# Experts taken in an order set by their token counts, two products instead of three for up and down in every second one, and every seventh weight remainder made by GpSimd

## The reference

```python
def moe_swiglu(h, w_router, w_gate, w_up, w_down):
    """Top-2-of-8 routed SwiGLU (softmax over the selected logits)."""
    logits = (h @ w_router).astype(jnp.float32)
    top_val, top_idx = lax.top_k(logits, TOP_K)
    top_w = jax.nn.softmax(top_val, axis=-1)
    ...
    for e in range(N_EXPERTS):
        y = swiglu(h, w_gate[e], w_up[e], w_down[e])
        out = out + gates[..., e:e + 1].astype(h.dtype) * y
    return out
```

## Time and profile before

| | us |
|---|---|
| median of 3 runs | 1777.85 (1777.68 to 1777.86) |
| span of the profiled execution | 1775.3 |
| TensorE matmuls busy | 1761.8 |
| VectorE busy | 1402.3 |
| ScalarE busy | 1141.6 |
| GpSimd busy | 134.5 |
| the experts | from about 443.5 to 1423 |

### The profile page before, as it was taken

One profiled execution on the slowest core, in us unless ns is written; L12 is line 12 of the kernel. 1 busy time (PEld: TensorE's weight loads), 2 busy tenths in 40 slices (PEclk: granted clock), 3 DMA queues, 4 the chain that ended last, 5 costly groups with the idle time before them and its releaser, 6 DMA issues.

```text
span 1775.3 us, 25580 instructions
## 1 busy us (share of the span) xinstructions
PE 1761.8 (99%) x9850; PEld 1525.6 (86%) x9850; DVE 1402.3 (79%) x1179; ACT 1141.6 (64%) x974; POOL 134.5 (8%) x142
## 2 busy tenths in 40 slices
PE   9999999999999999999999999999999999999999
PEld 8889999998888888888888888888888889789998
DVE  7475545655988989889889889898898879878775
ACT  6444433563777778777778777777777646756553
POOL 7000000000110000000000000000000017610000
PEclk9999999999999999999999999999999999999999
DMA  7447555542999999998999989999989943416561
GB/s 259 150 145 233 168 193 189 168 142 99 347 378 329 378 378 343 385 370 321 379 373 359 376 318 375 369 355 388 367 322 378 329 159 123 139 65 221 168 212 48
DMA packets 244645, 479.27 MB, mean 270 GB/s; under 512 B 11791, under 2 KB 80169, under 8 KB 244537
## 3 DMA queue, kind: packets, MB, share of 16 engines
q1 hardware_dynamic: 243673, 476.43, 75.1%
q10 hardware_dynamic: 864, 1.31, 0.2%
HBM read 476.66 MB, written 1.05 MB: 269 GB/s over the span
## 4 chain that ended last, share of the span: by engine, by line
PE 91%; DVE 4%; POOL 2%; ACT 1%; issue 1%; DMA 0%; DVEq 0%; ACTq 0%; SPq 0%; POOLq 0%
PE bank L2140 26%; PE bank L2142 26%; PE bank L2141 26%; PE bank L2648 1%; PE bank L2254 1%; PE bank L2262 1%; PE bank L2255 1%; PE bank L2591 1%; POOL arena L857 1%; POOL arena L856 1%; DVE xT L1410 1%; DVE wl L449 0%; PE bank L2436 0%; PE bank L2440 0%; PE bank L2437 0%
## 5 line engine op out<-in xcount | busy, mean ns | idle before, releaser
L1652 DVE TENSOR_TENSOR wl<-raw,wh 128x2048 fp32r<-128x2048 f32 x224 | 514.6, 2304 | 89.3 <-ACT wh L1082 88.1
L1082 ACT ACTIVATE wh<-raw 128x2048 fp32r<-128x2048 f32 x224 | 429.7, 1919 | 131.8 <-PE bank L2142 126.5
L2140 PE MATMUL bank<-wh,xTh 128*128 128x512 f32 x1000 | 395.9, 396 | 0.1
L2142 PE MATMUL bank<-wh,xTl 128*128 128x512 f32 x1000 | 389.8, 390 | 0.0
L2141 PE MATMUL bank<-wl,xTh 128*128 128x512 f32 x1000 | 389.1, 389 | 0.0
L449 DVE TENSOR_TENSOR wl<-raw,wh 128x2048 fp32r<-128x2048 f32 x112 | 254.8, 2292 | 65.4 <-ACT wh L442 63.6
L2140 PE MATMUL bank<-xTh,wh 128*128 128x256 f32 x944 | 268.0, 284 | 0.2 <-DVE wl L449 0.2
L2142 PE MATMUL bank<-xTh,wl 128*128 128x256 f32 x944 | 267.1, 283 | 0.0
L2141 PE MATMUL bank<-xTl,wh 128*128 128x256 f32 x944 | 267.1, 283 | 0.0
L1652 DVE TENSOR_TENSOR wl<-arena,wh 128x2048 fp32r<-128x2048 f32 x112 | 255.2, 2284 | 0.0
L1082 ACT ACTIVATE wh<-arena 128x2048 fp32r<-128x2048 f32 x112 | 215.3, 1922 | 50.4 <-PE bank L2142 50.3
(11 more groups left out here) (450 smaller groups left out, 2078.0 us busy)
## 6 DMA issues: line engine op xcount, KB each, us to landing
raw<-in_moe_w_up SPq DMA_DIRECT2D x112, 1024.0 KB, 7.6
arena<-in_moe_w_gate SPq DMA_DIRECT2D x96, 1024.0 KB, 7.4
raw<-in_moe_w_down SPq DMA_DIRECT2D x96, 1024.0 KB, 7.0
raw<-in_w_up SPq DMA_DIRECT2D x22, 1024.0 KB, 5.2
raw<-in_moe_w_gate SPq DMA_DIRECT2D x16, 1024.0 KB, 7.4
arena<-in_moe_w_down SPq DMA_DIRECT2D x16, 1024.0 KB, 7.1
raw<-in_gla_w_in SPq DMA_DIRECT2D x12, 1024.0 KB, 7.5
raw<-in_w_in SPq DMA_DIRECT2D x12, 1024.0 KB, 6.5
```

The lines of the kernel that those rows point to most:

```text
L1082: V.activation(wh[:, s, :], src, ACT.Copy).then_inc(sg("hi_moe"), 1)
L1652: V.tensor_tensor(wl[:, s, :], moe_raw(c)[0], wh[:, s, :].bitcast(F32), ALU.subtract).then_inc(lo_moe, 1)
L2140: T.matmul(o, xh, yh, start=first, stop=False)
L2142: return T.matmul(o, xl, yh, start=False, stop=last)
```

## The change

Four things are changed together.

1. After the router, VectorE sorts the experts by their counts. Expert 0 stays first; of the other seven, the four with the fewest tokens take the second place of the four pairs, the rest the first places. Gates and places in `pm` are permuted by the same matrix, and SyncE reads the number of the expert to load from `order_i`.
2. The second expert of a pair has 64 places (`CAP`). Its one-hot repeats the 64 columns, so that the gathered tile holds the tokens twice. For up and down the stationary operand is now 64 columns of the high part beside 64 columns of the low part (`BOTH`), and `mm2` multiplies it by w_high and by w_low: two matmuls in place of three. Gate keeps three. The two halves of the up result are added when the activation is turned, as a matmul with `fold`, and the halves of the down result when it is added back.
3. A further pass of four pairs runs where an expert has more than 128 tokens or at least four of experts 1 to 7 have more than 64.
4. Pieces c with c % 42 % 7 == 5 (six of an expert's 42) have their remainder made by GpSimd, which counts them in a semaphore of its own; its four `xnl` remainders are placed ahead of the first four of them. On GpSimd some small constants are added early in the kernel.

```diff
-        xTh = sb("xTh", [P, KD, S], F32R)
-        xTl = sb("xTl", [P, KD, S], F32R)
+        xhl = sb("xhl", [P, 2, KD, S], F32R)
+        xTh, xTl = xhl[:, 0], xhl[:, 1]
...
+        lo_moe_pool = sg("lo_pool")
+        pool_makes = [c % UC % 7 == 5 for c in range(PC)]
+        N_POOL = sum(pool_makes)
+        assert not any(pool_makes[0:NW])
+
         def moe_split(eng, at, c):
 
-            eng.wait_ge(lo_moe, at(PC, c + 1))
+            same = [k for k in range(c % PC + 1) if pool_makes[k] == pool_makes[c % PC]]
+            n = N_POOL if pool_makes[c % PC] else PC - N_POOL
+            eng.wait_ge(lo_moe_pool if pool_makes[c % PC] else lo_moe, at(n, c // PC * n + len(same)))
...
+        CAP = (P, P // 2)
+
         def slots(i):
 
             return slice((1 - i % 2) * P, (2 - i % 2) * P)
+
+        def tokens_of(i):
+
+            return xhl[:, 1 - i % 2]
+
+        HIGH, LOW, BOTH = slice(0, P), slice(P, 2 * P), slice(P // 2, 3 * P // 2)
+
+        def turned_act(i):
+
+            return bank[4][:, 0:4 * CAP[i]].rearrange("p (k s) -> p k s", k=4)
...
-                load_expert(c, 0)
+                load_expert(c, (0, 0))
             sp.wait_ge(sg("more_ready"), 1)
             more = sp.value_load(more_i[0:1, 0:1], min_val=0, max_val=NPAIR)
+            sp.wait_ge(sg("more_ready"), 2)
+
+            def expert_at(u):
+                return sp.value_load(order_i[0:1, bass.ds(u, 1)], min_val=0, max_val=NE - 1)
+
             with sp.Fori(0, more + (NPAIR - 1)) as p:
-                e = (p % NPAIR) * 2
+                e = expert_at(2 * (p % NPAIR)), expert_at(2 * (p % NPAIR) + 1)
                 for c in range(NRX, PC):
                     moe_split(sp, lambda a, b: p * a + b, c - NRX)
                     load_expert(c, e)
-                e2 = ((p + 1) % NPAIR) * 2
+                e2 = (expert_at(2 * ((p + 1) % NPAIR)),)
...
+            def weight_low(at, c):
+                s = (M0 + c) % NW
+                pool.wait_ge(sg("hi_moe"), at(PC, c + 1))
+                V.tensor_tensor(wl[:, s, :], moe_raw(c)[0], wh[:, s, :].bitcast(F32), ALU.subtract).then_inc(lo_moe_pool, 1)
+
+            mine = [c for c in range(PC) if pool_makes[c]]
+            for n, c in enumerate(mine):
+                if n < 4:
+                    pool.wait_ge(sg("moe_used"), 6 * n + 4 - 3 * (n > 0))
+                    xn_low(n)
+                weight_low(lambda a, b: b, c)
+            more = pool.value_load(more_i[0:1, 0:1], min_val=0, max_val=NPAIR)
+            with pool.Fori(0, more + (NPAIR - 1)) as p:
+                for c in mine:
+                    weight_low(lambda a, b: p * a + (a + b), c)
...
                 s = (M0 + c) % NW
+                if pool_makes[c % PC]:
+                    return
...
                 pmu = pm[:, bass.ds(u, 1), :].rearrange("p a t -> p (a t)")
-                V.tensor_tensor(oh2[:, :, slots(i)], iota2, pmu.unsqueeze(2).to_broadcast([P, TT, P]), ALU.is_equal).then_inc(sg("moe_oh"), 1)
+                n = CAP[i % 2]
+                shape = [P, TT, P // n, n]
+                V.tensor_tensor(oh2[:, :, slots(i)].rearrange("p t (a s) -> p t a s", s=n),
+                                iota[:, 0:n].unsqueeze(1).unsqueeze(1).to_broadcast(shape),
+                                pmu.unsqueeze(2).unsqueeze(3).to_broadcast(shape), ALU.is_equal).then_inc(sg("moe_oh"), 1)
...
+            C(V.memset(count[:, 0:1], -1.0))
+            C(V.tensor_reduce(cmax[0:1, 0:1], ct[0:1, 0:NE], AX.X, ALU.max))
+            C(V.tensor_copy(count[:, 1:NE], ct[:, 1:NE]), frees="cnt")
+            C(V.tensor_scalar(over[0:1, 1:NE], count[0:1, 1:NE], CAP[1] + 0.5, None, ALU.is_gt))
+            C(V.tensor_reduce(cmax[0:1, 1:2], over[0:1, 1:NE], AX.X, ALU.add))
+            C(V.tensor_scalar(cmax[0:1, 0:1], cmax[0:1, 0:1], CAP[0] + 0.5, None, ALU.is_gt))
+            C(V.scalar_tensor_tensor(cmax[0:1, 0:1], cmax[0:1, 1:2], NPAIR - 0.5, cmax[0:1, 0:1], ALU.is_gt, ALU.max))
+            C(V.tensor_scalar(more_i[0:1, 0:1], cmax[0:1, 0:1], float(NPAIR), None, ALU.mult), "more_ready")
...
                 moe_lo_one(at_first, c)
+
+            def in_order():
+
+                c1, c2, r = cmp1[:, 0], cmp2[:, 0], rank[:, 0, :]
+                ce, cj = count.unsqueeze(2).to_broadcast([P, NE, NE]), count.unsqueeze(1).to_broadcast([P, NE, NE])
+                C(V.tensor_tensor(c1, ce, cj, ALU.is_gt))
+                C(V.tensor_tensor(c2, ce, cj, ALU.is_equal))
+                C(V.tensor_tensor(c2, c2, tri8[:, :, :], ALU.mult))
+                C(V.tensor_tensor(c1, c1, c2, ALU.add))
+                C(V.tensor_reduce(r, c1, AX.X, ALU.add))
+                C(V.tensor_tensor(perm, place[:, :].unsqueeze(2).to_broadcast([P, NE, NE]),
+                                  r.unsqueeze(1).to_broadcast([P, NE, NE]), ALU.is_equal))
+                C(V.tensor_tensor(c1[0:1], perm[0:1], iota[0:1, 0:NE].unsqueeze(1).to_broadcast([1, NE, NE]), ALU.mult))
+                C(V.tensor_reduce(over[0:1, :], c1[0:1], AX.X, ALU.add))
+                C(V.tensor_copy(order_i[0:1, :], over[0:1, :]), "more_ready")
+                p4 = perm.unsqueeze(1).to_broadcast([P, TT, NE, NE])
+                for src, dst in ((lg, cmp1), (ex, cmp2)):
+                    C(V.tensor_tensor(dst, src.unsqueeze(2).to_broadcast([P, TT, NE, NE]), p4, ALU.mult))
+                C(V.tensor_reduce(lg, cmp1, AX.X, ALU.add))
+                C(V.tensor_reduce(ex, cmp2, AX.X, ALU.add))
+                lu = lg.rearrange("p t (a two) -> p two a t", two=2)
+                pu = pm[:, 0:2 * NE, :].rearrange("p (k a two) t -> p k two a t", k=2, two=2)
+                for k in range(2):
+                    for i in range(2):
+                        C(V.tensor_scalar(pu[:, k, i], lu[:, i], -1.0 - CAP[i] * k, None, ALU.add))
+                    C(V.tensor_copy(gt[:, k * NE:(k + 1) * NE, :], ex.rearrange("p t e -> p e t")))
+
+            in_order()
...
+                        low = eactTh[:, ks, CAP[1]:P] if i else eactTl[:, ks, :]
                         dve.wait_ge(sg("moe_actTh"), at(2 * NEJ, n + 1))
-                        V.tensor_tensor(eactTl[:, ks, :], bank[4][:, :].rearrange("p (k s) -> p k s", k=4),
-                                        eactTh[:, ks, :].bitcast(F32), ALU.subtract).then_inc(sg("moe_actTl"), 1)
+                        V.tensor_tensor(low, turned_act(i), eactTh[:, ks, 0:CAP[i]].bitcast(F32),
+                                        ALU.subtract).then_inc(sg("moe_actTl"), 1)
...
+            def mm2(o, x, yh, yl, first, last):
+
+                T.matmul(o, x, yh, start=first, stop=False)
+                return T.matmul(o, x, yl, start=False, stop=last)
...
-                            ins = mm3(b[:, :], xTh[:, kk, slots(i)], xTl[:, kk, slots(i)], h_[:, k, :], l_[:, k, :],
-                                      kk == 0, kk == KD - 1)
+                            if kind == "u" and i == 1:
+                                ins = mm2(b[:, :], x[:, kk, BOTH], h_[:, k, :], l_[:, k, :], kk == 0, kk == KD - 1)
+                            else:
+                                ins = mm3(b[:, :], x[:, kk, HIGH], x[:, kk, LOW], h_[:, k, :], l_[:, k, :],
+                                          kk == 0, kk == KD - 1)
...
-                            ins = T.transpose(bank[4][:, k * P:(k + 1) * P], eact[:, n % 2, k * P:(k + 1) * P], ident[:, :])
+                            block_ = eact[:, n % 2, k * P:(k + 1) * P]
+                            if i == 0:
+                                ins = T.transpose(bank[4][:, k * P:(k + 1) * P], block_, ident[:, :])
+                            else:
+                                ins = T.matmul(bank[4][:, k * CAP[1]:(k + 1) * CAP[1]], block_, fold[:, :], start=True, stop=True)
                         ins.then_inc(sg("moe_Tfull"), 1)
+
+                    def down_part(o, kk, yh, yl, first, last):
+                        if i == 0:
+                            return mm3(o, eactTh[:, kk, :], eactTl[:, kk, :], yh, yl, first, last)
+                        return mm2(o, eactTh[:, kk, :], yh, yl, first, last)
...
-                                    ins = mm3(bank[5 + half][:, :], eactTh[:, kk, :], eactTl[:, kk, :], h_[:, k, hs], l_[:, k, hs],
-                                              j == 0 and part == 0 and k == 0, False)
+                                    ins = down_part(bank[5 + half][:, :], kk, h_[:, k, hs], l_[:, k, hs],
+                                                    j == 0 and part == 0 and k == 0, False)
```

More of the change, by code:

```diff
@@ L101, in build @@
         iota = sb("iota", [P, P])
+        fold = sb("fold", [P, 64])
+        place = sb("place", [P, NE])
         tri8 = sb("tri8", [P, NE, NE])
@@ L546, in build @@
         more_i = ar(1).bitcast(I32)
+        order_i = ar(NE).bitcast(I32)
+        count, over = ar(NE), ar(NE)
+        perm = ar(NE * NE).rearrange("p (u e) -> p u e", u=NE)
         ghot, gnow = ar(1), ar(TT)
@@ L807, in _ @@
```

(29 more changed lines are left out.)

33 lines of the change are left out of this document (16 added, 17 removed).

## The result

The changed kernel takes 1794.22 us (median of 4 runs, 1794.06 to 1795.33) against 1777.76 us before: the ratio is 1.0095, 95% interval 1.0081 to 1.0109. It is slower by 16.5 us, where 1773 us was forecast. The profiled execution has a span of 1792.3 us, 17.0 above that of before.

The account below looks back on a forecast made before the run. TensorE was taken to bound the kernel, VectorE and DMA within 12% of it; +5.1 (start), +6.0 (first experts) and -15.6 (second experts) gave -4.5 us on the 1775.3 us span, about 1773 us, range 1730 to 1815.

Parts of the forecast that it names:

- Matmuls removed: Up and down of second experts lose 112 matmuls each expert, 25.4 us; TensorE alone would need 96.5 us.
- VectorE and GpSimd add up: Weight remainders on the two engines do not overlap, so VectorE's 92.1 us and GpSimd's 27.2 us are added.
- rival (a): GpSimd's remainders cost VectorE nothing and DMA sets the pace: 1711 to 1750 us; chance 0.22.
- Second experts, 118.1 us, a gain of 3.9 each: Second experts paced by VectorE plus GpSimd, 118.1 us in place of 122.0; four times, 15.6 us gained.
- First experts, +1.5 each: First experts of the pairs: VectorE's slack used up, 1.5 us charged each for misses, 6 in all; bounds 0 and 6 each.
- rival (b): GpSimd is let in late, TensorE stalls 2.9 us at some pieces, its clock may fall: 1783 to 1850 us; chance 0.28.
- The start, +5, bounds 3 to 12: First expert: 19 small ordering instructions delay piece 4 (3.2 us stall), piece 5 waits behind xnl (1.9 us).
- Load before the order: nothing: SyncE's piece 6 load, now behind the order, lands some 5 us later, just meeting TensorE's later need; otherwise up to 10 us.
- The sum: Whole kernel: +5.1 start, +6.0 first experts, -15.6 second experts, -4.5 us on the span; about 1773 us, 0.3% faster.
- (c): The further pass of four more pairs runs, about 2750 us; chance 0.02.
- (d): Second experts gain nothing because an unseen limit holds their pace, the start's cost remains: 1783 us; chance 0.06.
- DMA's 112.9 us, named as the next limit: Weight loads: 42 pieces an expert at 390 GB/s allow at best 112.9 us, unless pieces are already there.

Follow-up runs that it names:

- run 1: Changed kernel with no weight remainders on GpSimd, ordering and two products kept: 1755.8 us, 0.9873 of the kernel before.
- run 2: Kernel before the change with only GpSimd's weight remainders added, no ordering, three products everywhere: 1793.53 us, 1.0088.
- run 7: Changed kernel, GpSimd subtracting only 8 columns of its pieces and filling the rest with zeros (remainders lost): 1751.39 us, one execution.
- run 8: Changed kernel, GpSimd subtracting only 896 of the 2048 columns of its pieces, the rest not made: 1753.01 us, one execution.
- Run 9: Changed kernel, GpSimd waiting for VectorE's remainder of the piece in front before starting its own: 1784.29 us, 1.0045.
- run 3: As run 1, and SyncE loads expert 0 before the order is known: 1757.24 us, 0.9877.
- run 4: Changed kernel, GpSimd as in the change, with expert 0 loaded before the order is known: 1795.33 us, 1.0098.
- run 5: As run 3, with the order cut into five parts behind piece 12 and later ones, and VectorE's first pair unrolled: 1748.79 us, 0.9838.
- run 6: As run 1, second experts loading only half of each piece (results not the reference's): 1734.46 us, one execution.

## Why the prediction was wrong, step by step

No single term explains the miss: the gain of the second experts fell short by 8.9 us, the start cost 7.3 more and the first experts 4.5 more than put down. The step whose mechanism failed, and the one term whose total lies outside its bounds, is the start: it took VectorE's small instructions to run undisturbed beside GpSimd.

- **Matmuls removed.** 448 fewer follow from the change; the page has 336 fewer, and since some records can be missing the count is not confirmed. In second experts TensorE ceased to be the limit, with 13.4 us idle where 20 were forecast.
- **VectorE and GpSimd add up.** Right, shown by runs 1, 2, 7 and 8; rival (a) falls. The price of it was only seen in part: by the same sum the six pieces cost second experts more than they save (27.2 for 13.7 us), and without them the version of run 1 is faster than both kernels.
- **Second experts, 118.1 us, a gain of 3.9 each.** The length was right within 1 us (118.9 to 119.2). The gain was not: it was taken from windows of 122.0 us, that is 1.3 us too long for a second expert, which marks put at 120.7. It is 1.7 each, 6.7 in all, not 15.6. Of the 8.9 us between the two, 5.0 are how I cut the windows (4 x 1.26) and 3.9 are the 1.0 us by which the experts were longer than forecast.
- **First experts, +1.5 each.** Measured +1.6 to +2.4 in two and +6.5 in the fourth pair. Run 9 takes 3.7 off the last: GpSimd went first and VectorE's piece came late, at one place. The prediction had only the reverse, GpSimd let in late, as rival (b). The others are longer without the ordering too (by 1.5 to 1.8 us in run 2); TensorE's matmuls wait only 0.4 us for GpSimd in them, so where this time goes stays open.
- **The start, +5, bounds 3 to 12.** This is the step that failed: 12.4. I had seen VectorE's 4.7 us of small instructions, piece 5 behind xnl, and the late load, and priced the first two at 5.1. Run 1 shows 8.7 for the order alone and run 2 shows 9.1 for GpSimd alone. In the change TensorE stands once, for 10.2 us, and its first 3 us or so of work are done at half the clock, an estimated 1.6 us more: 11.8 of the 12.4. The sum had 3.2 us and 1.9 us of stall. The 4.7 us for the 19 instructions were right for instructions that wait for nothing (5.75 us in run 1, of which 1.0 is the copy beside the xnl remainder). What had no price: small SBUF instructions of VectorE wait for GpSimd's long ones (4.56 us for two that need 0.38 in run 1), 1.5 us behind them without work, and the clock, which stood in rival (b) only.
- **Load before the order: nothing.** Right by runs 3 and 4: without the late load nothing was gained. The 10 us for a case in which TensorE's need had not moved were not tested.
- **The sum.** By its own steps: -15.6 became -6.7, +6 became +10.5, +5.1 became +12.4; together -4.5 became +16.2; the rest of the 17.0 lies behind the last mark.
- **Rivals (b), (c) and (d).** The time, 1794 us, lies in (b)'s range of 1783 to 1850, but mostly by other causes: TensorE's matmuls waited for GpSimd's pieces about 5 us in each second expert and not over 0.4 us in any first one. The prediction called any such wait in a first expert a sign against it; at 0.4 us it decides nothing. No further pass ran (c), and second experts did gain (d); what ate the gain was the start and the first experts.
- Had the two products come without GpSimd, DMA's 112.9 us, named as the next limit, would have held: 113.0 to 114.8 measured.

## What to carry to other kernels

Before a second engine takes over part of a queue, ask whether the two can run at the same time with the operands they have; if not, the sum of both, not the larger, is the time (118.1 us by the sum, 118.9 to 119.2 measured), and a slower helper makes it longer. What was put in front of the first pieces of this pipeline, four slots deep, cost more than its length (8.7 us for 5.75 us of instructions in run 1); from piece 12 on, in parts of 0.6 to 2.2 us, it cost nothing (run 5). Cut windows by a mark that recurs, not by equal lengths, before two kinds of stage are compared.

## What the runs showed of the hardware that I had not expected

- The block is not one of weight remainders only: a `tensor_scalar` of 128 x 8 and a copy of 128 x 16, which have a single input, waited beside GpSimd's subtraction (4.56 us for two, 1.20 for one). For the `tensor_scalar` pair writing alone is enough, unlike for a weight remainder. In run 7 it took 2.00 us and ended 0.04 us after GpSimd's memset, which reads nothing:

```profile
456.89 2.00 DVE L1814 TENSOR_SCALAR arena<-arena 128x8 f32<-128x8 f32 x2
...
457.06 1.79 POOL L874 MEMSET wl<- 128x2040 f32 x1
```

- A start 0.14 us earlier decided which of two remainders went first, and then it held for 4.6 us (fourth pair of the change).
- In a stall of 10.2 us TensorE's granted clock went to 0.50 and stayed there for the first 3 us of work; in second experts, with TensorE busy 89%, the mean was 0.96 to 0.97.
- From the last instruction ahead of its loop to the first in it VectorE let 1.50 to 1.51 us pass in the change and in runs 1, 3, 4, 6, 7, 8 and 9, each time with only short instructions in front. Whether the register read there or the loop itself takes the time is not separated.
